# A two-layer decoder step: attention reordered and rebuilt, conditioning multiplied without a split and moved

## What is computed

```python
sh1, sc1, g1, sh2, sc2, g2 = split(silu(c) @ ada_w[layer] + ada_b[layer], 6)   # the conditioning
h = rmsnorm(x) * (1 + sc1) + sh1
# layer 0:  x += g1 * gla(h);  x += g2 * swiglu(h2);  then k, v = split(adaLN(x) @ kv_w)
# layer 1:  q = h @ w_q
z = q @ k.T * 64**-0.5 + bias                      # per head, 16 heads of 64
log1m = where(key < query, log_sigmoid(-z), 0)
later = reverse_cumsum(log1m) - log1m
out = exp(where(key < query, log1m + z + later, -inf)) @ v
# x += g1 * (out @ w_out);  x += g2 * top2_of_8_experts(h2);  y = adaLN(x)
```

## Time and profile before

| | |
|---|---|
| median of 3 runs | 2048.81 us (2046.06 to 2053.83) |
| profiled execution | 2050.78 us, its span 2049.0 us |
| busy: PE / DVE / ACT / POOL | 92% / 74% / 61% / 5% |
| DMA | 518.85 MB, 253 GB/s over the span |
| chain that ended last | PE 77%, DVE 9%, ACT 5%, issue 5%, DMA 3% |

### The profile page before, as it was taken

How to read it: one execution, slowest core, us unless ns; L and a number is a source line. 1 busy time by engine, 2 the same in 40 slices (tenths; PEclk the granted TensorE clock), 3 DMA queues, 4 the chain that set the end, 5 groups by cost and what they waited for, 6 DMA issues and landing times.

```text
span 2049.0 us, 26624 instructions
## 1 busy us (share of the span) xinstructions
PE 1881.7 (92%) x9526; PEld 1463.5 (71%) x9526; DVE 1509.3 (74%) x1900; ACT 1251.3 (61%) x1490; POOL 102.5 (5%) x112
## 2 busy tenths in 40 slices
PE   5799996899999966886999999999999999999996
PEld 2696554888999733264787877878778787787784
DVE  5374777677555576354998989989899898898993
ACT  5553444566444434144777777777777777777773
POOL 2000010000000130001000000000000000000000
PEclk9897777999999868986999999999999999999998
DMA  9254784388544250451898989989989899899990
GB/s 310 86 189 153 254 295 147 124 273 273 203 177 157 91 206 1 168 191 64 318 358 305 360 329 333 362 319 340 364 300 359 325 335 366 302 356 336 329 350 21
DMA packets 233433, 518.85 MB, mean 253 GB/s; under 512 B 5188, under 2 KB 27818, under 8 KB 233363
## 3 DMA queue, kind: packets, MB, share of 16 engines
q1 hardware_dynamic: 229202, 504.42, 69.0%
q0 software_dynamic: 3856, 12.40, 1.6%
q10 hardware_dynamic: 304, 1.08, 0.2%
HBM read 509.91 MB, written 7.96 MB: 253 GB/s over the span
## 4 chain that ended last, share of the span: by engine, by line
PE 77%; DVE 9%; ACT 5%; issue 5%; DMA 3%; DVEq 0%; SPq 0%; POOL 0%; ACTq 0%; POOLq 0%
PE psum L610 19%; PE psum L611 18%; PE psum L612 18%; PE psum L582 3%; DMA ring<-in_moe_w_gate_up 3%; PE psum L583 3%; DVE w_lo L1375 2%; PE psum L955 2%; PE psum L853 2%; PE psum L970 1%; PE psum L600 1%; PE psum L777 1%; PE psum L715 1%; DVE x L1463 1%; ACT w_hi L1327 1%
## 5 line engine op out<-in xcount | busy, mean ns | idle before, releaser
L1790 DVE TENSOR_TENSOR w_lo<-ring,w_hi 128x1024 fp32r<-128x1024 f32 x672 | 815.9, 1224 | 120.8 <-ACT w_hi L1327 109.8
L1327 ACT CAST w_hi<-ring 128x1024 fp32r<-128x1024 f32 x672 | 704.3, 1053 | 231.0 <-PE psum L612 230.9
L1375 DVE TENSOR_TENSOR w_lo<-ring,w_hi 128x1024 fp32r<-128x1024 f32 (+1 forms) x260 | 311.2, 1215 | 204.2 <-ACT w_hi L1069 203.0
L1069 ACT CAST w_hi<-ring 128x1024 fp32r<-128x1024 f32 (+1 forms) x260 | 265.5, 1040 | 237.8 <-PE psum L583 110.5
L610 PE MATMUL psum<-w_hi,xe_hi 128*128 128x512 f32 x896 | 371.1, 414 | 4.3 <-DVE w_lo L1790 4.3
L612 PE MATMUL psum<-w_hi,xe_lo 128*128 128x512 f32 x896 | 354.6, 396 | 0.0
L611 PE MATMUL psum<-w_lo,xe_hi 128*128 128x512 f32 x896 | 354.3, 395 | 0.0
L610 PE MATMUL psum<-hh,w_hi 128*128 128x264 f32 x864 | 253.4, 293 | 21.7 <-DVE hl L1444 13.0
L611 PE MATMUL psum<-hl,w_hi 128*128 128x264 f32 x864 | 249.1, 288 | 0.0
L612 PE MATMUL psum<-hh,w_lo 128*128 128x264 f32 x864 | 249.0, 288 | 0.0
L610 PEld LDWEIGHTS psum<-w_hi,xe_hi 128*128 128x128 f32 x896 | 169.3, 189 | 41.9 <-DVE w_lo L1790 4.7
(11 more groups left out here) (300 smaller groups left out, 2088.1 us busy)
## 6 DMA issues: line engine op xcount, KB each, us to landing
ring<-in_moe_w_gate_up SPq DMA_DIRECT2D x112, 2048.0 KB, 7.9
ring<-in_moe_w_down SPq DMA_DIRECT2D x56, 2048.0 KB, 7.7
ring<-in_ada_w SPq DMA_DIRECT2D x24, 2048.0 KB, 9.8
ring<-in_ffn_w_gate_up SPq DMA_DIRECT2D x22, 1024.0 KB, 7.5
ring<-in_gla_w_in SPq DMA_DIRECT2D x6, 2048.0 KB, 7.9
ring<-in_kv_ada_w SPq DMA_DIRECT2D x4, 2048.0 KB, 10.4
ring<-in_ffn_w_down SPq DMA_DIRECT2D x4, 2048.0 KB, 7.8
ring<-in_kv_w SPq DMA_DIRECT2D x4, 2048.0 KB, 8.3
```

What stands on the lines that cost most here:

```text
L1069: eng.copy(unit(w_hi, kind, m, ks), quarter(slot(kind, i), kind, m % 4, ks)).then_inc(S["hi_ready"], 1)
L1327: eng.copy(unit(w_hi, kind, n), quarter(ring[(BASE + j // 4) % RING], kind, j % 4)).then_inc(S["hi_ready"], 1)
L1375: eng.tensor_tensor(unit(w_lo, kind, m, ks), quarter(slot(kind, i), kind, m % 4, ks), unit(w_hi, kind, m, ks), ALU.subtract).then_inc(S["l ...
L1790: eng.tensor_tensor(unit(w_lo, kind, n), quarter(ring[(BASE + j // 4) % RING], kind, j % 4), unit(w_hi, kind, n), ALU.subtract).then_inc(S ...
```

## The change

1. Conditioning: no split. `c_pad` holds `c` in 9 of 32 columns; the 8 row chunks of a tile are multiplied in plain fp32, chunk k into the 32-row strip k mod 4 of PSUM; a product with `strip_sum` instead of the transpose adds the four strips. Its slot is free when TensorE is done. The ada units leave `SPLIT`; where a stage begins after them, its first three units are split by `first_splits`.
2. Conditioning tiles 20 to 25 move from the feed-forward into the attention loop, 26 and 27 (and as before 28 to 31) to the router. Six stand behind the output projection, where four stood.
3. The queries are projected first, with the scale in ScalarE's copy, then K/V. The sample queries go to a scratch tensor in device memory and come back spread over 128 partitions (GpSimd's queue). Sample scores run on VectorE and GpSimd during the K/V projection, in place in the cache tile, and K/V are transposed in turns between its blocks. Cache tiles 0 to 2 of K share a slot.
4. In the attention, bias (fp32r, 1/64 times split bias) and mask (-1e30) are multiplied into PSUM ahead of the scores, the sums are added to the same banks with negated triangles, and ScalarE reads and exponentiates from PSUM. VectorE keeps one pass and the low half of the result.
5. Sample values: two samples at once, 4 strips (two halves of the heads by two samples), one page after the other, in groups 2, 3, 5 and 6 of the loop; `sel_own` sums own heads into transposed rows.

In this order: the list of tiles, TensorE's `ada`, GpSimd's queue, TensorE's projection and attention, VectorE's part during the K/V projection.

```diff
-          + [t for i in range(11) for t in ([("ffn_up", i)] + ([("ada", 19 + i)] if 1 <= i <= 8 else []))]
+          + [("ffn_up", i) for i in range(11)]
+          + [("sb_q", i) for i in range(2)]
+          + [("kv", 0), ("kv", 1), ("k_cache", 0), ("kv", 2), ("k_cache", 1), ("kv", 3), ("k_cache", 2), ("k_cache", 3)]
+          + [("ada", 20)] + [t for i in range(4) for t in (("ada", 21 + i), ("v_cache", i))] + [("ada", 25)]
+          + [("sb_out", i) for i in range(2)] + [("ada", i) for i in range(26, 32)])
+STAYS = {("k_cache", 1): ("k_cache", 0), ("kv", 3): ("kv", 1)}
+SPLIT = [t for t in STREAM if t[0] not in ("k_cache", "v_cache", "ada")]
+PAGES_DURING = {1: (0, 0), 2: (0, 1), 3: (1, 0), 4: (1, 1), 7: (0, 2), 8: (0, 3), 9: (1, 2), 10: (1, 3), 13: (0, 4),
+                14: (0, 5), 15: (1, 4)}
+PAGES_AFTER = ((1, 5), (0, 6), (0, 7), (1, 6), (1, 7))
+ADA_DURING = {0: 20, 1: 21, 3: 22, 4: 23, 6: 24, 7: 25}
+OWN_DURING = {2: 0, 3: 1, 5: 2, 6: 3}
...
-                    has_unit(n)
-                    for k in range(2):
-                        c = c_split[:, 2 * j + k, 0:CR]
-                        eng.matmul(to, c, unit(w_hi, "ada", n)[:, k, :], start=j + k == 0, stop=False)
-                        last = eng.matmul(to, c, unit(w_lo, "ada", n)[:, k, :], start=False, stop=j + k == 4)
+                    if j % 2 == 1:
+                        for g in range(STRIPS):
+                            k = (j // 2) * STRIPS + g
+                            last = eng.matmul(pb[ADA_BANKS[i]][g * STRIP:(g + 1) * STRIP, :], c_pad[:, k, :],
+                                              cols8(slot("ada", i))[:, k, :], start=j == 1, stop=j == 3)
...
+            eng.wait_ge(S["qs_kept"], 1)
+            eng.dma_start(q_scratch, qs_tok).then_inc(S["q_stored"], 16)
+            eng.wait_ge(S["q_stored"], 16)
+            eng.wait_ge(S["hl_ready"], (IN_KV + 1) * KC)
...
+            def load_q(b):
...
+                eng.dma_start(q_rows[b % Q_ROWS], q_scratch[b].partition_broadcast(P)).then_inc(S[f"q_row{b % Q_ROWS}_loaded"], 16)
...
+            project("kv", 4, IN_KV, then=lambda i: i in TURN_AFTER and turn_kv(TURN_AFTER[i]))
...
+                for a in range(2):
+                    eng.matmul(to[a][:, 0:384], sixty_fourth[:], bias_r[:, 2 * g + a:2 * g + a + 1].to_broadcast([P, 384]),
+                               start=True, stop=False, skip_group_check=True)
+                for a in range(2):
+                    eng.matmul(to[a][:, 0:256].rearrange("p (s t) -> p s t", s=2), ident_r[:],
+                               never[:].unsqueeze(1).to_broadcast([P, 2, P]), start=False, stop=False, skip_group_check=True)
...
             for g in range(G + 1):
                 if g < G:
                     later_sums(g)
+                if g in OWN_DURING and OWN_DURING[g] >= 1:
+                    own_rows(OWN_DURING[g] - 1, g - 1)
                 if g >= 1:
                     values(g - 1)
+                if g in ADA_DURING:
+                    ada(4 * ADA_DURING[g], 4 * ADA_DURING[g] + 4, ends=g == G - 1)
                 if g + 2 < G:
                     z_products(g + 2)
...
+                if g in OWN_DURING:
+                    values_s(OWN_DURING[g])
+            own_rows(NB // 2 - 1, G)
...
+            for u in range(16):
+                if u in PAGES_DURING:
+                    page, b = PAGES_DURING[u]
+                    (page1_scores if page else page0_scores)(b)
+                split(UNIT_AT["kv", 0] + u + AHEAD)
```

More of the change, by code:

```diff
@@ L79 @@
+SLOT_AT, BEFORE = [], []
+for tile in STREAM:
+    SLOT_AT.append(SLOT_AT[TILE_AT[STAYS[tile]]] if tile in STAYS else (SLOT_AT[-1] + 1) % RING if SLOT_AT else 0)
+    BEFORE.append(max((n for n, s in enumerate(SLOT_AT[:-1]) if s == SLOT_AT[-1]), default=None))
+BASE = SLOT_AT[-1] + 1
+LAST_IN = [max(n for n, s in enumerate(SLOT_AT) if s == (BASE + j) % RING) for j in range(RING)]
 PER_E = 21
 WORK = 13 * 1024 + 96
-SPLIT = [t for t in STREAM if t[0] not in ("k_cache", "v_cache")]
+WORK3 = WORK - 3 * P - SH
@@ L372, in _ @@
             for n, (kind, i) in enumerate(STREAM):
-                dst = ring[n % RING]
+                dst, landing = ring[SLOT_AT[n]], loaded[SLOT_AT[n]]
                 if kind == "ada" and 4 <= i < 4 + NB * PAGES:
@@ new lines, in values_s @@
+            def values_s(i):
+                landed(eng, "v_cache", i)
+                if i == 0:
+                    eng.wait_ge(S["exps_s"], 1)
+                    eng.wait_ge(S["att_consts"], 4 + 2 * STRIPS)
+                vt = slot("v_cache", i)
+                for page in range(PAGES):
+                    for g in range(STRIPS):
+                        a, odd = g % 2, g // 2
+                        lo = (odd * 2 + page) * D + a * 512
+                        last = eng.matmul(pb[5][g * STRIP:(g + 1) * STRIP, :], zs[:, page, 2 * i + odd, :], vt[:, lo:lo + 512],
+                                          start=page == 0, stop=page == PAGES - 1, skip_group_check=True)
+                        if page == PAGES - 1:
+                            last.then_inc(S["opv_done"], 1)
@@ L1094, in ada @@
                         ada_copy(i - 1)
-                    split(UNIT_AT["ada", i] + j + AHEAD)
                 if ends:
@@ L1277, in _ @@
-            eng.wait_ge(S["otT_kept"], 1)
-            eng.wait_ge(S["pv_kept"], G)
-            for k in range(KC):
-                eng.copy(hh[:, k, :], h[:, k, :]).then_inc(S["hh_ready"], 1)
+                    eng.copy(hh[:, g - 1, 0:TP], pb[4][:, 0:TP]).then_inc(S["hh_ready"], 1)
+                if g in ADA_DURING:
+                    ada(4 * ADA_DURING[g], 4 * ADA_DURING[g] + 4, ends=g == G - 1)
+                if g == 1:
+                    eng.wait_ge(S["abs_s"], 1)
+                    link(eng.activation(ls, ls, ACT.Exp, scale=-1.0))
+                    eng.activation(ls, ls, ACT.Ln, bias=1.0).then_inc(S["soft_s"], 1)
@@ L1281, in _ @@
+                if g == 2:
+                    eng.wait_ge(S["args_s"], 1)
+                    eng.activation(zs[:, :, :, 0:SH], zs[:, :, :, 0:SH], ACT.Exp).then_inc(S["exps_s"], 1)
+                if g + 2 < G:
+                    soft(g + 2)
+            eng.wait_ge(S["os_done_all"], NB // 2)
+            eng.copy(hh[:, :, TP:T], rows_s).then_inc(S["os_hi"], 1)
+            first_splits("sb_out")
             split_during("sb_out", 2)
-            norm(FFN1, splits=False, after=(S["kept_dve"], empt[-1][1]), during=(112, 116))
@@ L1284, in _ @@
-            ada(116, 124)
+            norm(FFN1, splits=False, after=(S["kept_dve"], empt[-1][1]), during=(104, 108))
+            ada(108, 120)
             eng.wait_ge(S["gates_exp"], 1)
             eng.activation(e2[:, 0:TT], e2[:, 0:TT], ACT.Exp).then_inc(S["gates_exp_done"], 1)
-            ada(124, 128, ends=True)
+            ada(120, 128, ends=True)
             eng.wait_ge(S["most_ready"], 1)
```

556 lines of the change are left out of this document (267 added, 289 removed).

## The result

The changed kernel takes 1950.1 us (median of 4, 1944.2 to 1955.2), the kernel before 2049.9 us beside it (median of 4, 2046.1 to 2053.8): a ratio of 0.951, 95% interval 0.949 to 0.954. It is faster, as forecast, but by 100 us and not by 153; 1950.1 lies just above the upper end of the range. The profiled execution took 1950.4 us, its span 1948.7. The page of the changed kernel has these lines against the earlier trace rows: busy time and, in the second line, the granted clock in tenths over 40 equal slices.

What follows compares the result with a forecast made beforehand. TensorE, working through its queue in order and 92% busy, was taken as the bound. Stage terms summed to -153.5 us: 2050.8 - 153.5 = 1897 us; own span 1870 to 1925, full range 1855 to 1950.

Steps and rivals of the forecast that it cites:

- feed-forward: Dense feed-forward: eight conditioning tiles leave at 4.19 us each and nothing comes in; -34 us (-36 to -30).
- start: Before the first squares' sum: no units split there any more, but ACT waits for the first GLA tile; -6 us (-12 to -3).
- strips' price: Conditioning tiles: eight fp32 multiplies in four strips side by side take 2.2 us a tile at full clock, 3.7 at half.
- rival C: Conditioning and sample value rounds: strips run one after another; near 2240 us at half clock (3%), near 2030 at full (4%).
- B: Attention: TensorE waits for each tile passing three ring slots, 9.5 us a group; +20, +5 in the projection, 1922 us; 20%.
- D: Changes between strips and full array drain TensorE: 0.1 us each, 11 us in all; at 0.27, 30 us and 1922; 8%.
- the states: Sample states, nine tiles: an iteration falls from 9.9 to some 8 us; -9 us (-25 to +10).
- rival A: GLA chunks and sample states: the clock stays at 1.2 GHz; chunks +3, states +10, so +30 and 1927 us; 15%.
- E: All goes well: full clock in chunks and states (-20), few stalls of DVE (-15); 1862 us; 12%.
- Queries to attention: From the queries to the end of attention: 168 us become 87, with attention groups of 7 us; -81 us (-105 to -50).
- term (b): KV projection: DVE's splits queue behind sample scores awaiting the query row; stalls some 10 us, 9 us of scores shown after.
- Router: Router: 16 unit splits of 1.2 us leave ACT and DVE, two more tiles are loaded; -10 us (-14 to +4).

Runs made afterwards that it cites:

- one-strip run: Changed kernel with all eight multiplies of a conditioning tile accumulated into one strip, the other three unused: 2037.9 us (one run).
- early query: Changed kernel with sample queries copied before the keys/values norm and the first query row loaded into its own buffer: 1948.7 us (one run).
- short broadcasts: Sample states' two fp32 value broadcasts made two plus two fp32r multiplies: 1942.4 us on the changed kernel, 1923.9 with transposes for the strip sum (one run each).

## Why the prediction was wrong

**Right, and by the steps named.** The feed-forward (-34.5 for -34), the start (-7.9 for -6), the output norm (-6.2 for -5.5), the experts untouched. The strips' price, taken from the pairs in the earlier trace rows, held to 5%. That the one-strip run came within 8 us of rival C's lesser case was luck, as said with it: two errors cancel. B is refuted: in the attention no wait of TensorE for a ring slot shows, and with the transposes its groups go at DMA 0.94 busy without one. D's small price, 0.1 us a change, is near the 0.15 at most that the changed kernel's rows leave.

**The term that was left out: the sum over the strips.** The step "I take 2.2 us a tile at full clock, 3.7 at half" costs the eight strip multiplies and lets the turn pass as part of it ("new near 3 with its turn", "conditioning 2.2 x 6/8"). The change named it (point 1: a product with `strip_sum`): four fp32 multiplies, full stationary, nine columns. They measured 1.06 and 1.88 us a tile, so a tile is 3.2 and 5.8 us. Doing it by transposes gave back 41.5 us of the 53 missed. In the profiled executions, 45.1 us apart, it is 30.9 in the states, 4.6 in the chunks (76.1 to 71.5), 4.6 in the attention and 5.9 in the router, with 2.0 lost at keys and values. In the states the sum's own time, nine times 1.88, is 17 us of the 24.6 missed; the run with a quarter of it confirms 12.7 of these and 6.6 more. With the transposes the states are 15.3 us shorter than before, where 9 were forecast.

**The clock, seen as a rival and priced too low.** A round of the states was forecast at 8 us, and at 10.7 should the clock stay down (rival A, 15%); it was 12.75 as shown above: strips 3.9 (priced 3.7), broadcasts 3.8 (4.0), one-column multiplies 3.6 (3.0), and 1.9 for the sum (0), less what they overlap. So A happened in the states, and with the sum on top they came to +15.6 where A had +10; in the chunks it happened in part, at a clock of 0.68 after 0.75. "Against: four strips fill the array" was the argument for giving it 15%, and it was no row: the before's 0.77 was there with 16 multiplies of 512 columns a round, and the change took half of them. With the eight multiplies of a tile one after another in one strip the clock was 0.85. The range's upper end was built of A, B and D; the missing term moves all of them up by some 40 us, and so the result fell on its edge. (The lower end is given as E's 1855, but E's own sum is 1862.)

**Queries to attention, +12.7.** Two parts. Attention 69.9 us where 63 was summed (56 and 7): 6 x 1.06 = 6.4 us is the strip sum. Keys and values with the scores +5.8: the mechanism of term (b) was right, with waits of 5.8 us on TensorE and 8.3 on DVE for the query row, but its size, "some 10 us" and 9 shown behind, was short by about as much as the early query gives back, 6.9.

**Router, +10.** The 16 splits, "of which half stood between the squares' sum and the gates", were credited with the gain, but TensorE's tiles are the path. Four of the six stand between logits and gates and take 22 us, 5.5 each, in a stage at 0.61 of the clock; the forecast looked only at when the last of them lands. Moving the four away took 20.2 us off, moving the two others 4.8.

**What stays open.** What within a round makes the clock go up or stay down: less work in it lowered the clock once (short broadcasts after the transposes, 0.69 to 0.53) and raised it once (a quarter of the sum, 0.50 to 0.56). And up to 5 us of chunks differ from run to run with the same code. So do the states: with the transposes and otherwise the same code they took 77.6, 80.8 and 83.5 us in three kernels, at clocks of 0.69, 0.66 and 0.63, so that what is told from single profiled executions there is good to some 6 us.

## What to carry to other kernels

Cost every instruction that a diff adds, the small ones that tie two large steps together above all: here four multiplies a tile of nine columns each, done by transposes, gave 41 us beside the 100 of the whole change. Where the profile shows a stage at 0.5 to 0.8 of TensorE's clock, a forecast by durations is good only as long as the mix of the stage stays; price it at half clock throughout as the upper bound, and carry that bound into the range together with the others. And look at a tile's place before moving it: on the path it was worth 5 us, beside a norm 2.4.

## What the runs showed of the hardware that was not expected

TensorE busy for 99% of a stage (107.4 of 108.6 us, 1.1 us of waiting) can have half its clock throughout: the granted clock is 0.50 from 191.9 to 325.0 us. Less work can also be slower: with the transposes and the short broadcasts TensorE was busy for 86.6 us in the stage, with the transposes alone for 76.0. Four fp32 multiplies of 512 columns in four column strips took 1.06 us, in one strip 3.62, a factor of 3.4. The Trainium skill (TensorE: Matmul & The Clock Gate, the section on packing small matmuls) has 2.38 for three strips. The forecast's estimate from it for four, 2.6 us a tile, was too high: 2.1 were measured. And DVE's eight products of 1024 columns (L1690) ran beside POOL's in every case: three of them took 1.23 us, and POOL's beside these 3.4; the other five took 2.2 to 3.6, and POOL's beside most of these 2.4. So the two hold each other up, and either of them can be the one that pays.
